# Chunk scores in column groups, tables and states asked for later, multiplicities as four rows, slab requests first, two waits moved

## The reference

```python
mod = silu(c) @ w_ada + b_ada              # shift, scale, gate of both sub-layers
h   = rmsnorm(x) * (1 + scale1) + shift1
qa, ka, va, qb, kb, vb, r, glr = split(h @ w_in)          # 6160 columns
log_a = log_sigmoid(glr @ w_gate2 + b_gate2) / 16
oa  = dilated window attention, 16 heads of 64, windows (128,1), (512,4), (2048,16), with
      a shared relative bias; sample tokens also read cache_k_win and cache_v_win (1024 rows)
ob  = GLA, 4 heads, dk 128, dv 256:  state = exp(log_a) * state + k v;  o = q state
      (prompt in chunks; sample from state_gla)
x  += gate1 * ([rmsnorm(oa), rmsnorm(ob) * silu(r)] @ w_out)
h   = rmsnorm(x) * (1 + scale2) + shift2
g, u = split(h @ w_up);  x += gate2 * ((silu(conv3(g)) * u) @ w_down)
```

## Time and profile before

| | |
|---|---|
| time, median of 3 runs | 1621.52 us (1619.14 to 1622.28) |
| the profiled execution | 1621.12 us, its span 1619.6 us |
| TensorE busy | 1582.2 us (98%) |
| VectorE busy | 890.9 us (55%) |
| ScalarE busy | 664.2 us (41%) |
| GpSimd busy | 76.9 us (5%) |
| moved | 370.81 MB, mean 229 GB/s |

### The profile page before, as it was taken

How to read it: one execution, slowest core, us unless ns; L and a number is a source line. 1 busy time by engine, 2 the same in 40 slices (tenths; PEclk the granted TensorE clock), 3 DMA queues, 4 the chain that set the end, 5 groups by cost and what they waited for, 6 DMA issues and landing times.

```text
span 1619.6 us, 29366 instructions
## 1 busy us (share of the span) xinstructions
PE 1582.2 (98%) x12352; PEld 1430.2 (88%) x12352; DVE 890.9 (55%) x1504; ACT 664.2 (41%) x925; POOL 76.9 (5%) x135
## 2 busy tenths in 40 slices
PE   8899999999999998999999999999999999999997
PEld 4677888888877765997999999999999999999997
DVE  3555555555665654657445455454555556656563
ACT  3332333343445434435334333343433445545452
POOL 2010000000111000000000000000000000000000
PEclk8999999999999999999999999999999999999999
DMA  9998877778877999866644444555545455555450
GB/s 339 375 384 298 307 258 260 270 278 282 288 255 278 335 397 368 310 231 235 229 163 158 158 161 156 182 163 175 161 158 168 148 170 179 160 177 179 158 183 27
DMA packets 240881, 370.81 MB, mean 229 GB/s; under 512 B 7809, under 2 KB 192483, under 8 KB 232553
## 3 DMA queue, kind: packets, MB, share of 16 engines
q1 hardware_dynamic: 216032, 279.88, 51.1%
q10 hardware_dynamic: 17538, 71.45, 11.8%
q0 software_dynamic: 7184, 17.64, 3.3%
HBM read 359.06 MB, written 9.88 MB: 228 GB/s over the span
## 4 chain that ended last, share of the span: by engine, by line
PE 83%; DMA 5%; issue 5%; DVE 4%; ACT 2%; SPq 1%; POOL 0%; ACTq 0%; POOLq 0%; DVEq 0%
PE ps L949 23%; PE ps L950 22%; PE ps L951 22%; PE ps L900 3%; PE ps L1197 2%; DMA ring<-in_w_in 1%; DMA ring<-in_w_ada 1%; DMA vals<-in_w_ada 1%; SPq L548 1%; DMA proj<-in_w_ada 1%; DVE wlo L2041 1%; PE ps L1212 1%; PE ps L1243 1%; PE ps L893 1%; DMA ring<-in_w_out 1%
## 5 line engine op out<-in xcount | busy, mean ns | idle before, releaser
L949 PE MATMUL ps<-hhi,whi 128*128 128x288 f32 x3120 | 929.7, 298 | 1.7 <-DVE hlo L2033 0.7
L950 PE MATMUL ps<-hlo,whi 128*128 128x288 f32 x3120 | 917.8, 294 | 0.0
L951 PE MATMUL ps<-hhi,wlo 128*128 128x288 f32 x3120 | 917.6, 294 | 0.0
L949 PEld LDWEIGHTS ps<-hhi,whi 128*128 128x128 f32 x3120 | 586.0, 188 | 40.1 <-issue 35.3
L950 PEld LDWEIGHTS ps<-hlo,whi 128*128 128x128 f32 x3120 | 586.2, 188 | 0.8
L951 PEld LDWEIGHTS ps<-hhi,wlo 128*128 128x128 f32 x3120 | 586.0, 188 | 0.0
L1897 DVE TENSOR_TENSOR wlo<-ring,whi 128x1024 fp32r<-128x1024 f32 x178 | 212.2, 1221 | 84.7 <-ACT whi L1479 84.3
L1479 ACT ACTIVATE whi<-ring 128x1024 fp32r<-128x1024 f32 x178 | 184.5, 1056 | 156.3 <-PE ps L951 156.3
L2041 DVE TENSOR_TENSOR wlo<-ring,whi 128x1024 fp32r<-128x1024 f32 x96 | 117.2, 1223 | 124.2 <-ACT whi L1488 124.0
L1488 ACT ACTIVATE whi<-ring 128x1024 fp32r<-128x1024 f32 x96 | 100.8, 1054 | 157.5 <-PE ps L951 125.4
L2541 DVE TENSOR_TENSOR wlo<-ring,whi 128x1024 fp32r<-128x1024 f32 (+1 forms) x94 | 105.7, 1131 | 56.0 <-ACT whi L1817 56.0
(11 more groups left out here) (318 smaller groups left out, 1115.7 us busy)
## 6 DMA issues: line engine op xcount, KB each, us to landing
ring<-in_w_up SPq DMA_DIRECT2D x88, 1024.0 KB, 5.1
ring<-in_w_ada ACTq DMA_DIRECT2D x58, 1024.0 KB, 7.2
ring<-in_w_in SPq DMA_DIRECT2D x48, 1024.0 KB, 8.8
ring<-in_w_down SPq DMA_DIRECT2D x32, 1408.0 KB, 6.6
ring<-in_cache_k_win SPq DMA_DIRECT2D x16, 1024.0 KB, 9.3
ring<-in_w_out SPq DMA_DIRECT2D x16, 1024.0 KB, 7.0
proj<-in_w_ada SPq DMA_DIRECT2D x14, 1024.0 KB, 9.4
ring<-in_w_ada SPq DMA_DIRECT2D x10, 1024.0 KB, 13.6
```

Of the source, the lines that this page charges most:

```text
L949: mm(out, w_hi, x_hi, start=start, stop=False)
L950: mm(out, w_hi, x_lo, start=False, stop=False)
L951: return mm(out, w_lo, x_hi, start=False, stop=stop)
```

## The change

1. The tables are cut up. SyncE's first load takes the first 393 of 817 constant columns; the causal and batch masks come by GpSimd later (`masks_in`). The multiplicities of the past keys (640 columns by 128 rows) become four rows (`mult_t`), which TensorE adds with a product with a 4-row selection `pick_t`; VectorE then copies instead of adding.
2. GpSimd asks for the masks, the gate columns, w_gate2 and state_gla after `turn_b` 3 and not after `turn_b` 2. `gate_rank`, the copy of its result and `keep_ones` come one iteration later.
3. In `att` the 32 queries of a chunk stand still, in the column group c % 4, and up to 256 keys move: eight products for each head. Their result is queries by keys; ScalarE copies it (`att_rows`) and TensorE transposes it in three products at the end of step 5.
4. The sum of squares waits for `state_half`, the second of the last four states; the next head's z waits for `state1`.
5. `idle_products(2, 6)` becomes `idle_products(2, 2)`.
6. In ScalarE's loop `late_rows`, `lead_load` and `late_load` come before `in_hi(j + 3)`.

```diff
...
     t = np.arange(TS)
+    add("pick_t", (t[:, None] == r[None] % TS).astype(np.float32))
+    add("mult_t", multiplicity(PAST + t[:, None] - pos[None]))
     add("hot_s", np.concatenate(
         [np.concatenate([one_hot(PAST + k - pos), one_hot(k - a % TS)], 1) for k in t], 0))
-    old = multiplicity(PAST + t[:, None] - pos[None])[r % TS]
     new = []
     for g in range(NB // 2):
         b = 2 * g + r // 64
         m = multiplicity((r % TS)[:, None] - (a % TS)[None])
         new.append(np.where(b[:, None] == a[None] // TS, m, NEG))
-    add("mult_s", np.concatenate([old] + new, 1).astype(np.float32))
+    add("mult_s", np.concatenate(new, 1).astype(np.float32))
     return np.concatenate(parts, 1)
...
 
-            sp.dma_start(con[:, :], a["tables"][:, 0:keep]).then_inc(con_in, 16)
+            sp.dma_start(con[:, 0:front], a["tables"][:, 0:front]).then_inc(con_in, 16)
 
...
             pool.wait_ge(full[1], 16)
-            c1 = CONST_LAYOUT["hot_s"][0]
-            pool.dma_start(temp[0:NBUCK, 0:c1 - c0], a["tables"][0:NBUCK, c0:c1]).then_inc(temp_in, 16)
+            c1, ct = CONST_LAYOUT["hot_s"][0], CONST_LAYOUT["pick_t"][0]
+            pool.dma_start(temp[0:NBUCK, 0:ct - c0], a["tables"][0:NBUCK, c0:ct]).then_inc(temp_in, 16)
+            pool.dma_start(temp[0:TS, ct - c0:c1 - c0], a["tables"][0:TS, ct:c1]).then_inc(temp_in, 16)
             pool.dma_start(temp[:, c1 - c0:], a["tables"][:, c1:cn[0] + cn[1]]).then_inc(temp_in, 16)
...
             pool.wait_ge(btab_out, 16)
-            pool.wait_ge(*AT.upto("turn_b", 2))
+            pool.wait_ge(*AT.upto("turn_b", 3))
             pool.wait_ge(fill_c, 1)
+            pool.dma_start(con[:, front:keep], a["tables"][:, front:keep]).then_inc(masks_in, 16)
             pool.dma_start(wglr[:, :, 0:RANK], w_in[:, :, 6144:6160]).then_inc(wglr_in, 16)
...
 
-                pe.wait_ge(temp_in, 32)
+                pe.wait_ge(temp_in, 48)
                 pe.wait_ge(rel_in, 64)
                 pe.wait_ge(*PV_.upto("x15"))
                 mm(ps[0:H_A, 0, :], relb[0:NBUCK, :], tview("hot_p", NBUCK), start=True,
                    stop=True).then_inc(*PT_.step("bias_p"))
                 pe.wait_ge(*PV_.upto("rel_rows"))
-                mm(ps[:, 1, :], rel_rows, tview("hot_s", P)[:, 0:512], start=True, stop=True)
-                mm(ps[:, 2, 0:160], rel_rows, tview("hot_s", P)[:, 512:672], start=True,
+                mm(ps[:, 1, :], rel_rows, tview("hot_s", P)[:, 0:512], start=True, stop=False)
+                mm(ps[:, 1, :], tview("pick_t", TS), tview("mult_t", TS)[:, 0:512], start=False, stop=True)
+                mm(ps[:, 2, P:P + NS], rel_rows, tview("hot_s", P)[:, CK:CK + NS], start=True, stop=True)
+                mm(ps[:, 2, 0:P], rel_rows, tview("hot_s", P)[:, 512:CK], start=True, stop=False)
+                mm(ps[:, 2, 0:P], tview("pick_t", TS), tview("mult_t", TS)[:, 512:CK], start=False,
                    stop=True).then_inc(*PT_.step("bias_s"))
...
                 pe.wait_ge(*RV.upto(f"ki{c}", h))
-                q = qp[:, 32 * c:32 * c + 32]
-                n = min(P, 32 * (c + 1))
-                last = mm(ps[0:n, 7, 32 * c:32 * c + 32], ki[c % 4][:, 0:n], q, start=True, stop=True)
-                if c >= 4:
-                    n = 32 * (c - 3)
-                    last = mm(ps[0:n, 7, P + 32 * c:P + 32 * c + 32], ki[c % 4][:, P:P + n], q, start=True,
-                              stop=True)
-                last.then_inc(*RT.step(f"att{c}"))
+                at, n, rows = P * (c // 4), 32 * (c + 1), slice(32 * (c % 4), 32 * (c % 4) + 32)
+                mm(ps[rows, 7, at:at + n], qp[:, 32 * c:32 * c + 32], ki[c % 4][:, 0:n], start=True,
+                   stop=True).then_inc(*RT.step(f"att{c}"))
+
+            def att_turns(h):
+
+                pe.wait_ge(*RA.upto("att_rows", h))
+                for n in range(3):
+                    last = turn(ps[:, 7, P * n:P * n + P], att_rows[:, P * n:P * n + P], ident)
+                last.then_inc(*RT.step("att_turned"))
 
...
                     pe.wait_ge(wg2_in, 64)
+                    pe.wait_ge(*RV.upto("state1", h - 1))
                     mm(ps[:, 7, 0:TOK], wg2[:, P * h:P * h + P], glrT, start=True, stop=True).then_inc(*RT.step("z"))
...
                     last.then_inc(*RT.step("os_rows"))
+                    att_turns(h)
                 if r == 6:
...
                     pe.wait_ge(*RA.upto("sq", h))
-                    pe.wait_ge(*RV.upto("state1", h))
+                    pe.wait_ge(*RV.upto("state_half", h))
                     for e in range(2):
...
                     in_chunk(j)
-                if j == 24:
+                if j == 25:
                     gate_rank()
...
                 if i == 0:
-                    idle_products(2, 6)
+                    idle_products(2, 2)
                 for n in range(2):
...
                         scaled(c)
+                    act.wait_ge(*RT.upto("att7", h))
+                    f(att_rows, ps[:, 7, 0:384], ACT.Copy).then_inc(*RA.step("att_rows"))
                 if r == 6:
...
                     tile_copy(j // 4 - 1)
-                if j + 3 < CH_OUT:
-                    in_hi(j + 3)
+                if j - 1 in LATE_AT[KD - 1::KD]:
+                    late_rows(LATE_AT.index(j - 1) // KD)
                 for a_ in range(4, 24):
                     if ADA_AT[a_ - 4] == j - 1:
                         lead_load(a_)
                 for r in range(48):
                     if (LATE_AT[r - 2] if r >= 2 else ADA_AT[20 + r]) == j - 1:
                         late_load(r)
-                if j == 25:
+                if j + 3 < CH_OUT:
+                    in_hi(j + 3)
+                if j == 26:
                     act.wait_ge(*GT.upto("done"))
...
                     norm_hi(1 + ADA_AT[7::8].index(j - 2))
-                if j - 1 in LATE_AT[KD - 1::KD]:
-                    late_rows(LATE_AT.index(j - 1) // KD)
                 for h in range(H_B):
...
                 ms = tview("mult_s", P)
-                v.tensor_tensor(bias_s[:, 0:512], ps[:, 1, :], ms[:, 0:512], ALU.add)
-                v.tensor_tensor(bias_s[:, 512:CK], ps[:, 2, 0:P], ms[:, 512:CK], ALU.add).then_inc(*PV_.step("bias_s0"))
+                v.tensor_copy(bias_s[:, 0:512], ps[:, 1, :])
+                v.tensor_copy(bias_s[:, 512:CK], ps[:, 2, 0:P]).then_inc(*PV_.step("bias_s0"))
                 new = ps[:, 2, P:P + NS].rearrange("p (a c) -> p a c", a=1).to_broadcast([P, 4, NS])
                 v.tensor_tensor(bias_s[:, CK:].rearrange("p (g c) -> p g c", g=4), new,
-                                ms[:, CK:].rearrange("p (g c) -> p g c", g=4), ALU.add).then_inc(*PV_.step("bias_s"))
+                                ms.rearrange("p (g c) -> p g c", g=4), ALU.add).then_inc(*PV_.step("bias_s"))
 
...
                 if r == 6:
-                    dve.wait_ge(*RT.upto("att7", h))
+                    dve.wait_ge(masks_in, 16)
+                    dve.wait_ge(*RT.upto("att_turned", h))
                     v.tensor_tensor(attT, ps[:, 7, 0:384], causal, ALU.mult).then_inc(*RV.step("att"))
...
                         last = new_state(b)
+                        if b == 5:
+                            last.then_inc(*RV.step("state_half"))
                     last.then_inc(*RV.step(f"state{r - 7}"))
...
```

More of the change, by code:

```diff
@@ L91, in constants @@
     add("ones", np.ones((P, P), np.float32))
+    add("sum_groups", (np.arange(P)[:, None] % 32 == np.arange(NC9)[None]).astype(np.float32))
     s, c = np.arange(P)[:, None], np.arange(SEQ)[None]
@@ L97, in constants @@
     add("own_batch", np.tile((a[:, None] // TS == np.arange(NB)[None]).astype(np.float32), (P // NS, 1)))
-    add("sum_groups", (np.arange(P)[:, None] % 32 == np.arange(NC9)[None]).astype(np.float32))
     dist = 2 * P - 1 - np.arange(512)
@@ L159, in build @@
         work = sb("work", [P, 2048])
-        keep = CONST_LAYOUT["sum_groups"][0] + NC9
+        front, keep = CONST_LAYOUT["causal"][0], CONST_LAYOUT["own_batch"][0] + NB
         con = sb("con", [P, keep])
@@ L253, in build @@
         ki = [projf[:, t:t + 256] for t in (1698, 1954, 6304, 6560)]
+        att_rows = projf[:, 1698:2082]
         rb = projf[:, 2210:2219]
@@ L304, in build @@
         x_in = [sem(f"x_half_in{n}") for n in range(2)]
-        con_in, c_in, vec_in, rel_in, temp_in, wglr_in, wg2_in, vrow_in = (
-            sem(n) for n in ("con_in", "c_in", "vec_in", "rel_in", "temp_in", "wglr_in", "wg2_in",
+        con_in, masks_in, c_in, vec_in, rel_in, temp_in, wglr_in, wg2_in, vrow_in = (
+            sem(n) for n in ("con_in", "masks_in", "c_in", "vec_in", "rel_in", "temp_in", "wglr_in", "wg2_in",
                              "vrow_in"))
@@ L363, in build @@
         RT = st("gla_tensor", "z", "vrows", "att_s", *(f"att{i}" for i in range(4)), "kdrows",
-                *(f"att{i}" for i in range(4, 8)), "state", "os_rows", "o", "states0", "states1", "sum")
```

(7 more changed lines are left out.)

## The result

The changed kernel took 1624.47 us in the median of 8 executions (1621.72 to 1627.66), the kernel before 1620.73: ratio 1.0021, interval 1.0012 to 1.0030. The two differ by 2 us for the same program. Over both, the changed kernel's mean is 1623.1 us, standard error 0.5 (20 executions); that of the kernel before, over the 87 executions beside runs e1 to e16, is 1621.4, error 0.2: 1.7 us slower.

The account below looks back on a forecast made before the run. TensorE, busy for 1582.2 of 1619.6 us, was taken as the bound; 0 - 1.6 - 1.4 - 1.9 - 1.5 + 0 + 5.8 = -0.6 gave 1620.5, rounded to 1620.8 us. The range was 1615.5 to 1625 us.

Parts of the forecast that it names:

- Late order, +5.8: ScalarE's later iterations, hi part behind late requests: 1.9 us each at j=74 and 86, 2.0 at four lesser places.
- Early requests and tables, -1.6 to chunk 8: First 90 us: slabs come 2.7 us earlier, partly given back as later hlo parts hold chunk 8; -1.6 us.
- Slab at 137, -1.4: TensorE's wait for the slab at 137 us goes once GpSimd's 64-byte-row loads move later; -1.4 us.
- States' waits, -1.5: Sum of squares waits for the second of four states, clearing both waits of 0.7 at L1119; -1.5 us.
- Heads, -1.9: Chunk scores in column groups, four heads: nominally -5.6 us, cut to -1.9 by waits for VectorE's keys.
- Idle products, 0: Before the first up chunk four idle products go, but VectorE's norm holds the third chunk behind; 0 us.
- Start, 0: Before the first chunk: slab 1.4 us earlier against 1.4 us of added products; 0, ends -0.9 and +1.0.
- The likeliest case: Whole kernel: no change, with its own range from 1618.3 to 1624.8 us; chance 0.44.
- a rival: TensorE's clock falls behind the waits at 431 and 492, a whole chunk each, +5.2: 1625.7 us; chance 0.22.

Follow-up runs that it names:

- e1: Changed kernel plus four idle products on TensorE in front of the fifth slab of w_ada; 1623.6 us, ratio 1.0023 to the kernel before.
- e16: Changed kernel with in_hi in front of the requests in iterations 74 and 86; 1618.07 us, ratio 0.9982 to the kernel before.
- the first comparison: Changed kernel, whole change, timed against the kernel before, 8 executions; 1624.47 us, ratio 1.0021.
- the second: Changed kernel once more, timed against the kernel before, 12 executions (e15); 1621.54 us, ratio 1.0007.
- e2: Changed kernel with late_rows and late_load back behind in_hi, lead_load still in front; 1612.4 us, ratio 0.9938 to the kernel before.
- e5: Kernel before with one edit, late_rows and late_load before in_hi in the late iterations; 1631.64 us, ratio 1.0069.
- e15: Changed kernel once more, unaltered, on one chip with e13, e14 and e16; 1621.54 us, ratio 1.0007 to the kernel before.
- e13: Changed kernel with the old tables (constants and multiplicities as before); 1624.53 us, ratio 1.0023 to the kernel before.
- e14: Changed kernel with old tables and in_hi in front of the requests in iterations 74 and 86; 1618.39 us, ratio 0.9984 to the kernel before.
- e7: Kernel before with the chunk scores in column groups alone; 1618.88 us, ratio 0.9981.
- e8: Changed kernel once more, unaltered, for one more trace of its clock; 1624.59 us in one execution.
- e9: e2 without the tables' part: constants loaded whole, multiplicities a full table that VectorE adds; 1615.45 us, ratio 0.9963 to the kernel before.
- e4: Kernel before with the cut tables and four-row multiplicities alone, masks loaded by GpSimd ahead of the gate columns; 1623.1 us, ratio 1.0011.
- The square on one chip: e13 to e16: changed kernel with tables old or new, late waits there or not; 1624.53, 1618.39, 1621.54 and 1618.07 us.
- e12: e2 unchanged, run once more; 1615.49 us, ratio 0.9960 to the kernel before.

## Why the prediction was wrong

It forecast no change, 1620.8, and the first comparison said slower, 1624.47, by 0.21%; with the second it is 0.1%. The range held both. By its own steps:

- **Late order, +5.8: right.** 1.9 at each of the two places (table above). From chunk 26 to 95 the changed kernel takes 361.25 us and e2, which differs in this alone, 352.82: 8.4, less the 1.7 of a fall of the clock near 524 us that e2's trace hasn't, so 6.7. Forecast were 5.8, and a delay of 1.9 against 1.2 of slack in two heads, which the prediction has within the heads' term. e5, the late order alone, has 7.6 over the same chunks.
- **Early requests and tables, -1.6 to chunk 8: right in size** where the start has no second stretch (e15: 46.86 to 88.42 against 46.44 to 89.89, so -1.9). In the changed kernel's own trace it is -3.0, and chunk 0 starts 5.5 us late there, which gives the slabs time to land. The reckoning missed the wait in front of chunk 3 that the requests first bring with the old tables (e13, e14); with the new ones it doesn't appear, so the sum holds and the shares of its two parts don't.
- **Slab at 137, -1.4: right**, -1.5. **States' waits, -1.5: right**; neither is left. **Heads, -1.9: right**: the four steps come to -1.4 in the changed kernel, whose first head waits 1.2 us at L1086 as the late order reaches it, and to -2.8 in e7. The drain of the Trainium skill's page "TensorEngine Tiling (Array Packing)" isn't seen there: the eight products in groups take 1.00 us from start to start, as before. **Idle products, 0: right**: products at 656.72 and 763.82 before stand at 659.17 and 766.26, the same 2.4 later.
- **Start, 0: wrong as a claim.** I read one trace of before and took its start as fixed. Chunk 0 starts between 45.9 and 46.9 in eight of the nineteen traces and from 48.2 to 53.0 in the others, which have a second stretch or a longer first one. The changed program's three traces have chunk 26 at 173.80, 172.83 (e8) and 169.77 (e15): the two with a second stretch are 3 to 4 us late.
- **The step that failed is the one that left the clock out of the sum.** The likeliest case had TensorE at full clock behind both waits and its start fixed, and only a rival had it otherwise: a whole chunk at the lower level behind each wait, +5.2, or nothing at all. Measured, it is a chance at each wait, 5 of 12 at 1.7 us each, so 1.4 us in an execution; and a chance in the start, 2.4 us in the mean of the three traces of the changed program, reckoned from that of e15. (The rival's price was off as well: a chunk is 24 products here, not 72 as said ahead of the prediction, and takes 3.2 us, from 427.23 to 430.39 for chunk 75 before, not 2.6.)

The steps without the clock are -3.3 at chunk 26 (e15), +2.4 from there to 95 (changed against before, which both have a fall near 524), and -0.7 between chunk 95 and 656 us, which no step forecast: -1.6 in all, where the forecast had -0.6. With the clock it is -1.6 + 1.4 + 2.4 = +2.2; measured over all executions is +1.7, standard error 0.5. These are few traces, so the sum shows that the clock is large enough, not more.

The first comparison had 3.5, its 8 executions having a clock of 0.9892; the 12 of e15 had 0.9908 and a ratio of 1.0007. That the time moved clear of the noise in the first comparison and not in the second is for the most part chance between executions.

The Trainium skill ("TensorE: Matmul & The Clock Gate", the part on oscillation in real kernels) tells of a kernel that waits some 3 to 5 us for transfers before each burst of products and drops to the lower clock every time. The waits here are shorter, 1.1 and 0.9 us with products between them, and they were followed by the fall at five places of twelve.

What stays open: whether the change makes the second stretch more likely. With all tables old one trace of six starts chunk 0 late (e9), with any of the new ones ten of thirteen; that speaks for it, and so does e4 with its lower clock. The square on one chip speaks against it, as the clocks over whole executions don't differ with the tables there. If the kernel before had such starts as often as the changed one, the 2.4 us would cancel, and nearly 2 us would be without a cause.

## What to carry to other kernels

An operation that is moved ahead of another one in a queue takes its wait along: what matters is not the issue time but who waits for the thing behind it. Here two steps of 1.9 us, with their clock, cost 5 to 6 us, and the whole late order 9, while all the other parts gain 7. Do such a move by place and not by rule: the late requests belong behind, and the early ones in front gained only with the new tables. And when TensorE is 98% busy, price a new wait of some 2 us with the chance that the clock falls behind it, read the granted clock of several executions before a start is taken as fixed, and take the cost of the clock from the place where it falls: a mean clock over the whole run also counts stretches in which TensorE has nothing to lose.

## What the runs showed of the hardware

- One program, same bytes and order, starts its first chunk at 46.7 us in one execution and at 53.0 in another (e2 and e12), by the stretches at the lower clock in its first 46 us. The times of e12's eight executions range over 10 us (1610.23 to 1619.96); how much of that comes from the start isn't shown, as one of them alone has a trace. Windows of e2 and then of e12 over these 46 us, mean clock 0.81 and 0.67 from 10 us on:

```profile
10.00:30.00 20.00, 20.00 (x106) 10.34 (x104) 10.80 (x40) 7.18 (x15) 2.63 (x6) 0.66 1.06 365
30.00:46.00 16.00, 15.82 (x86) 8.46 (x85) 6.83 (x16) 3.45 (x7) 0.50 (x1) 1.00 1.05 400
```

```profile
10.00:30.00 20.00, 18.06 (x103) 9.43 (x101) 11.20 (x41) 7.14 (x15) 2.63 (x6) 0.74 1.05 362
30.00:46.00 16.00, 15.95 (x54) 7.02 (x58) 3.03 (x5) 0.00 (x0) 0.50 (x1) 0.57 1.05 400
```

- Products with 32-column weights in column groups right behind full ones showed no drain: the eight at 254.19 take 1.00 us to the next start, as before.
- A wait of 2.1 us is followed by the lower clock in some executions of a kernel and not in others, at the same place and of the same length (5 of 12 such waits in six traces).
- A mean clock lower by 0.001 goes with 0.75 us more over 99 executions of the kernel before, half of what the span times the difference gives.
